# Score batches of two and three fills, a third one in the attention output's bank, and a scheduler with a readiness margin

## The reference

```
x  = layer_norm(x)                                   # entry norm
q,k,v,z_a,B,C,h,z_c = split(x @ w_in, 8)             # w_in 1024 x 4096, each part 512 wide
y_att  = chunk_attention(q,k,v,rel_bias) * silu(z_a) # 8 heads of 64; chunks of 64 frames;
                                                     # a chunk sees itself and 8 chunks before
y_conv = B * conv3(C*h) * silu(z_c)                  # causal depthwise conv of width 3
out = layer_norm(2**0.25 * x + concat(y_att, y_conv) @ w_out)
```

## Time and profile before

| | |
|---|---|
| median of 3 runs | 1316.02 us (1315.36 to 1316.21) |
| profiled execution | 1315.51 us |
| its span on the slowest core (core 2), first to last instruction | 1313.9 us |
| spans of the 8 cores | 1311.1 to 1313.9 us, granted PE clock 0.994 to 0.998 of full speed |
| PE busy | 1264.3 us (96%), 8146 matmuls recorded |
| DVE busy | 943.1 us (72%) |
| ACT busy | 731.4 us (56%) |
| POOL busy | 529.5 us (40%) |
| chain that ended last | PE 89% |

### The profile page before, as it was taken

The page is one execution under the profiler, slowest core; times in us unless marked ns, Lnnn a source line. Parts: engine busy times, 40 slices in busy tenths (PEclk is TensorE's granted clock), DMA queues, the critical chain, the costliest instruction groups (busy, mean ns, idle before and its releaser), DMA issues.

```text
span 1313.9 us, 27380 instructions; the slowest of 8 cores (1311.1 to 1313.9 us)
## 1 busy us (share of the span) xinstructions
PE 1264.3 (96%) x8146; PEld 594.9 (45%) x8308; DVE 943.1 (72%) x1671; ACT 731.4 (56%) x1082; POOL 529.5 (40%) x880
## 2 busy tenths in 40 slices
PE   5989999999999999999999999999999999999996
PEld 3434444444444444444444444444444444444443
DVE  2488987858678685876858688585885868676377
ACT  4665555555545565654654556465564565555563
POOL 4555533424343342433524334243443334334244
PEclk9999999999999999999999999999999999999998
DMA  9993313323222331222312323131222313221012
GB/s 290 322 254 113 88 55 93 89 49 89 58 77 79 87 89 25 88 83 73 89 41 73 89 74 96 59 87 41 83 87 73 89 43 89 69 76 49 13 70 73
DMA packets 126001, 117.16 MB, mean 89 GB/s; under 512 B 103200, under 2 KB 103200, under 8 KB 125728
## 3 DMA queue, kind: packets, MB, share of 16 engines
q1 hardware_dynamic: 125856, 115.40, 30.8%
HBM read 57.69 MB, written 33.55 MB: 69 GB/s over the span
## 4 chain that ended last, share of the span: by engine, by line
PE 89%; issue 3%; DMA 3%; DVE 2%; POOL 2%; ACT 1%; SPq 1%; POOLq 0%; DVEq 0%; ACTq 0%
PE mm L646 45%; PE mm L657 17%; PE mm L760 15%; PE pv L967 6%; PE sc L911 5%; DMA cst_sb<-cst 1%; DMA out<-xs 1%; DMA xs<-x 1%; DMA xnT<-xhb 0%; PE mm L833 0%; POOL pvs L985 0%; DVE stats L528 0%; DVE PT L951 0%; ACT xhb L855 0%; POOL rstd L538 0%
## 5 line engine op out<-in xcount | busy, mean ns | idle before, releaser
L646 PE MATMUL mm<-xnT,w_in_sb 128*128 128x512 bf16 x2970 | 709.3, 379 | 9.2 <-DVE tz L710 3.7
L646 PEld LDWEIGHTS mm<-xnT,w_in_sb 128*128 128x128 bf16 x3072 | 285.5, 98 | 300.6 <-issue 29.5
L924 ACT ACTIVATE PT<-sc 128x1024 bf16<-128x1024 f32 (+1 forms) x288 | 275.9, 999 | 115.6 <-PE sc L911 110.9
L657 PE MATMUL mm<-w_in_sb,xnT 128*128 128x512 bf16 x996 | 237.9, 379 | 1.9 <-issue 1.1
L760 PE MATMUL mm<-w_out_sb,yT 128*128 128x512 bf16 x929 | 221.5, 379 | 1.9 <-issue 1.3
L967 PE MATMUL pv<-vA,PT 128*128 128x65 bf16 x2240 | 203.3, 193 | 10.8 <-POOL PT L936 3.8
L967 PEld LDWEIGHTS pv<-vA,PT 128*128 128x128 bf16 x2240 | 150.2, 97 | 126.2 <-issue 18.6
L951 DVE TENSOR_TENSOR PT<-PT,etab 128x512 bf16<-128x512 bf16 (+1 forms) x304 | 123.6, 429 | 95.2 <-POOL PT L936 51.9
L985 POOL TENSOR_TENSOR pvs<-pvs,rden 128x256 f32<-128x256 f32 x128 | 100.7, 786 | 193.3 <-DVE rden L984 152.4
L657 PEld LDWEIGHTS mm<-w_in_sb,xnT 128*128 128x128 bf16 x1024 | 95.4, 98 | 105.7 <-issue 9.5
L766 DVE SCALAR_TENSOR_TENSOR xs<-xs,mm 128x512 f32<-128x512 f32 x120 | 82.2, 685 | 70.1 <-PE mm L760 59.1
(11 more groups left out here) (88 smaller groups left out, 1147.1 us busy)
## 6 DMA issues: line engine op xcount, KB each, us to landing
xs<-x SPq DMA_DIRECT2D x64, 512.0 KB, 3.6
out<-xs SPq DMA_DIRECT2D x60, 512.0 KB, 2.8
xs<-w_in SPq DMA_DIRECT2D x20, 512.0 KB, 12.8
g1bc_sb<-w_in SPq DMA_DIRECT2D x4, 512.0 KB, 12.7
b1bc_sb<-w_in SPq DMA_DIRECT2D x4, 512.0 KB, 12.8
vA<-w_in SPq DMA_DIRECT2D x4, 512.0 KB, 13.1
yT<-ytok SPq DMA_TRANSPOSE x128, 2.3
out<-xs SPq DMA_DIRECT2D x8, 256.0 KB, 2.0
```

Source lines behind the costliest of these rows:

```text
L646: P.op("pe", lambda e, i=i, kc=kc: e.matmul(mm[i][:, :], lhsT=w_in_sb[:, kc, c0:c0 + 128], rhs=xnT[:, sl, kc, :], start=(kc == 0), stop=(k ...
L657: P.op("pe", lambda e, i=i, kc=kc, t=t, c0=c0: e.matmul(mm[i][:, :], lhsT=xnT[:, sl, kc, t * 128:(t + 1) * 128], rhs=w_in_sb[:, kc, c0:c0 ...
L924: P.op("act", lambda e, x=x, sp=sp, w=w: e.activation(out=PT[:, sp, :, 0:w], in_=sc[x][:, :, 0:w], func=AF.Exp, scale=0.125), reads=["sc%d ...
```

## The change

Four things are changed together.

1. The PSUM banks are laid out anew. There are three score buffers `sc0`, `sc1`, `sc2` of two banks each and two `mm` banks. The two banks of `sc2` are also the third `mm` buffer and `pv`. A pair's five fills are now made in two batches: the first two in `sc0` and `sc1`, the last three in `sc2`, `sc0`, `sc1`. That is eight batches a block, and four in a block that starts a sequence. `pick` keeps units off the third `mm` buffer when their position lies from 14 before to 9 behind a batch of three; `place` moves such a batch by up to 12 positions (a position is one unit matmul) to where, by its count, the units are delayed least.
2. The scheduler's assumed times are changed: latencies between engines, durations on POOL, the DMA rate. A released operation that isn't PE's counts as ready later by 0.2 of what its deadline lies beyond 8 us, at most 3 us behind a DMA and 0.3 us behind an engine's operation. Zeroing the corner of `PT` may go to POOL or DVE.
3. The last output projection: its first two units leave out their last k chunk at first (that of the last convolution output) and add it after both have done the other seven. The last tile is made in units of 512, 256 and 256 columns, and its layer norm takes mean and variance with `bn_stats` on DVE instead of with ACT's squares; DVE finishes both halves.
4. Casts of weights and tables keep their choice of ACT or POOL; with the new assumed times, 19 of the 40 weight casts stand on ACT, where 7 stood before.

```diff
+FRAC = 0.5
+BEFORE = 14
+AFTER = 9
-LAT = 0.1
-DMA_MB = 0.3
+HOLD = {"pe": 0.0, "act": -0.09, "dve": -0.08, "pool": 0.17, "sp": 0.0}
+def lat(a, b):
+    if b == "pe":
+        return 0.145
+    return 0.16 if "pool" in (a, b) else 0.1
+DMA_MB = 0.31
+RISK = {"dma": 3.0, "sp": 1.5, "op": 0.3, "share": 0.2, "free": 8.0}
...
-                    ready[m] = max(ready[m], end + LAT)
-                    solid[m] = max(solid[m], end + LAT)
+                    to = nodes[m]["eng"]
+                    r = end + lat(e, to)
+                    if to != "pe":
+                        most = RISK["dma"] if e == "sp" else RISK["sp"] if to == "sp" else RISK["op"]
+                        r += min(most, max(0.0, RISK["share"] * (nodes[m]["alap"] - r - RISK["free"])))
+                    ready[m] = max(ready[m], r)
+                    solid[m] = max(solid[m], r)
...
-    mm = [ps("mm%d" % i, [128, 512], F32) for i in range(NMM)]
+    sc = [ps("sc%d" % i, [128, 2, 512], F32) for i in range(3)]
+    mm = [ps("mm%d" % i, [128, 512], F32) for i in range(2)] + [sc[2][:, 0, :]]
-    sc = [ps("sc%d" % i, [128, 2, 512], F32) for i in range(2)]
-    pv = ps("pv", [128, 2, 2, 65], F32)
+    pv = sc[2][:, 1, 0:260].rearrange("p (a b c) -> p a b c", a=2, b=2)
+    scr = [["sc0"], ["sc1"], ["mm2", "pv"]]
...
+    def pick(ord_, p):
+        for i in ord_:
+            if i < 2 or not any(p - AFTER < w < p + BEFORE for w in wide):
+                break
+        ord_.remove(i)
+        ord_.append(i)
+        return i
...
-                    P.op("pool", lambda e, sp=sp, c0=c0: e.memset(PT[0:64, sp, :, c0:c0 + 64], 0.0),
-                         writes=rs, us=0.2)
+                    fn = lambda e, sp=sp, c0=c0: e.memset(PT[0:64, sp, :, c0:c0 + 64], 0.0)
+                    P.any_op({"pool": (fn, 0.2), "dve": (fn, 0.2)}, writes=rs)
...
-        nbat = (len(fl) + 1) // 2
-        S = 8 * nu / nbat if nxt is not None else 8 * (nu - LU) / (nbat + 0.3)
+        S = 8 * nu / 4 if nxt is not None else 8 * (nu - LU) / 4.15
-        for k in range(nbat):
-            at(k * S, lambda k=k: qk_batch(fl[2 * k:2 * k + 2], b))
         for p in range(4):
-            z = max(n for n, f in enumerate(fl) if f[0] == p) // 2 * S
+            mine = [f for f in fl if f[0] == p]
+            z = p * S
+            if has_prev:
+                at(z, lambda two=mine[:2]: qk_batch(two, b))
+            z += FRAC * S
+            z = place(units, z, p * S + 8)
+            at(z, lambda three=mine[-3:]: qk_batch(three, b))
...
+    def o_last(b):
+        order = (4, 5, 6, 0, 1, 2, 3, 7)
+        pair = [next_mm(), next_mm()]
+        for hf in range(2):
+            o_mm(b, 0, pair[hf], hf * 512, 512, order[:7], True, False)
+        for hf in range(2):
+            o_mm(b, 0, pair[hf], hf * 512, 512, order[7:], False, True)
+            o_sum(b, 0, hf, pair[hf])
+        ln1_last(b, 0)
...
+        for k, (c0, w) in enumerate(((0, 512), (512, 256), (768, 256))):
+            i = next_mm()
+            o_mm(b, t, i, c0, w, order, True, True)
+            P.op("dve", lambda e, i=i, c0=c0, w=w: e.tensor_tensor(
+                out=xs[:, s, c0:c0 + w], in0=xs[:, s, c0:c0 + w], in1=mm[i][:, 0:w], op=ALU.add),
...
+        ln1_end(b, t, s)
```

More of the change, by code:

```diff
@@ L824, in build, with o_mm @@
     ybuf = xnT[:, :, :, :].rearrange("p s k c -> p (s k c)").bitcast(F32).rearrange("p (t d) -> p t d", d=D)
-    def unit_O_last(b, t, hf):
+    def o_mm(b, t, i, c0, w, chunks, first, last):
+        for n, c in enumerate(chunks):
+            assert (yc_of[c - 4] if c >= 4 else yt_of[c // 2, t]) == b
+            P.op("pe", lambda e, c=c, n=n: e.matmul(
+                mm[i][:, 0:w], lhsT=yT[:, c, t * 128:(t + 1) * 128], rhs=w_out_sb[:, c, c0:c0 + w],
+                start=(first and n == 0), stop=(last and n == len(chunks) - 1)),
+                reads=["w_out%d" % c, ("yT%d_%d" % (c // 2, t)) if c < 4 else "yT%d" % c],
+                writes=["mm%d" % i], us=w / 2400.0 + 0.0024)
+            pos_now[0] += 1
+            pump_pv(3)
@@ L903, in qk_batch @@
         sl = b % 2
-        for x, (pair, grp) in enumerate(batch):
+        bank = [2, 0, 1] if len(batch) == 3 else [0, 1]
+        for x, (pair, grp) in zip(bank, batch):
             coff = 0
@@ L1052, in build, with gated, place @@
     acts = set()
+    slow = set()
+    def gated(g):
+        slow.add(id(g))
+        return g
+    def place(units, z, lowest):
+        best = None
+        for shift in (0, 2, -2, 4, -4, 6, -6, 8, -8, 10, -10, 12, -12):
+            w = z + shift
+            if w < lowest or w > 8 * len(units) - 4:
+                continue
+            wide.append(base[0] + w)
+            ord_, late = list(mmo), 0.0
+            free = [0.0] * NMM
+            for n, g in enumerate(units):
+                p = 8.0 * n
+                i = pick(ord_, base[0] + p)
+                start = max(p + late, free[i])
+                if p - 8 < w <= p:
+                    late += max(0.0, free[2] - w - late)
+                    free[2] = w + late + 9
+                    start = max(p + late, free[i])
+                late = start - p
+                free[i] = start + 8 + (9.5 if id(g) in slow else 6)
+            late += 0.002 * abs(shift)
+            wide.pop()
+            if best is None or late < best[0]:
+                best = (late, w)
+        wide.append(base[0] + best[1])
+        return best[1]
     def block(b):
```

107 lines of the change are left out of this document (66 added, 41 removed).

## The result

The changed kernel takes 1302.13 us, the median of 4 runs (1301.55 to 1303.1), against 1316.08 us (1315.36 to 1316.21, 4 runs) before: ratio 0.9894, 95% interval 0.9879 to 0.9908. Forecast were 1300.7 us, 1294 to 1309. The sum was nearly right; of its terms one was right, two were too large, one had the wrong sign and one was missing.

A forecast was written before the change was run, and what follows sets the result against it. The prediction took PE as the bound, with next to nothing left to wait for. Its terms -9.0 + 1.5 - 7.2 - 0.6 = -15.3 us gave 1300.2 from the profiled 1315.5, so a median of 1300.7 us, range 1294 to 1309.

The forecast's parts named there:

- The runs of score matmuls: On PE, 45 fewer runs of score matmuls, each costing 0.2 us whatever its length: -9.0 us.
- The price of three: At the 64 batches of three, PE sometimes waits for the shared bank's evacuation: +1.5 us, bounds 0 and 16.
- The waits: Nine PE waits behind the first matmuls partly go, less 2.5 us for new ones: -7.2 us, bounds -12.6 and +5.
- the gate's: Two PE waits for a gate's evacuation, at 75.45 and 84.34 us, go: 4.0 us taken off.
- the pv buffer's: One PE wait for the pv buffer's evacuation, POOL being late with casts in between: 1.5 of 2.5 us taken off.
- the corner's waits: Five PE waits for the zeroed corner of PT, with 98 of 192 zeroings now on DVE: 3.0 of 4.6 us off.
- the bias product's: One PE wait for a bias product, behind statistics that wait for a load of x: 1.2 of 1.6 us off.
- I put back 2.5 us for new waits of the same kind: Allowance for new PE waits in the new order, set against the 9.7 us taken off: 2.5 us.
- PE gets to it after two units, so I leave 0.5 for it: Scaling of the second block's input comes later, behind the gate's evacuations: 0.5 us, within the 2.5 put back.
- The end: Last projection to program end: a 0.6 us wait goes and the rest stays 25.0 us; -0.6, bounds -4 and +2.
- Nothing but the runs: Rival: the waits are only moved, leaving the gains of -9.0 and -0.6: 1306.4 us, chance 0.22.
- ACT can't keep up: Rival: evacuations stand behind exponentials on ACT at batches of three, 16 to 22 us of PE waits: 1328.4 us, chance 0.08.

The follow-up runs named there:

- the batches alone: Changed kernel with the old scheduler numbers, zeroing on POOL and the old last projection: 1310.45 us, ratio 0.9949 to the kernel before.
- 64 runs put back: Changed kernel with each batch of three cut in two, its third fill one place later: 1316.01 us, ratio 0.9990 to the kernel before.
- without the margin: Changed kernel with no putting-off of ready times by deadline slack (share 0): slower than the kernel before, 16.3 us more lost on PE than in the changed kernel.
- loads earlier: Changed kernel with the weight loads' due times 3 us earlier: 1306.51 us, ratio 0.9922 to the kernel before.
- 1 MB more: Changed kernel with the two 0.5 MB residual-scaling tables also loaded once about 30 us after the start: 1312.0 us, ratio 0.9959 to the kernel before.
- tables held back: Changed kernel, margin off in PE's last 40 us, tables and w_out loads waiting for the second block's four input transposes: 1315.34 us, ratio 0.9984 to the kernel before.

## Why the prediction was right or wrong

- **The runs of score matmuls: right.** Predicted -9.0; -8.1 between the traces, -8.2 with the batches alone, 12.1 for 64 runs put back. An edge comes out at 0.18 to 0.19 us by these differences and at 0.21 at single places, which is the 0.20 assumed.
- **The price of three: wrong as a term of its own.** Predicted +1.5. In the changed kernel it is 0: no wait of PE from 160 to 1250 us. I argued from ACT's room and did not look at DVE, which evacuates the shared bank for the gates and for ubuf; without the margin the batch waited 10.4 us for it. Whether the price is paid is decided by what stands ahead of an evacuation, and the term belonged with the waits. On the Trainium skill, TensorEngine Tiling (Array Packing), section PSUM Bottleneck: between 550 and 630 us PE is busy for 80.00 of 80 with the larger batches, so no run here shows the reading of PSUM as a limit. Where a batch did wait for an evacuation, the evacuation itself took 0.68 us, and it was what stood ahead of it that made it late.
- **The waits: too large.** Predicted -7.2, and together with the price of three -5.7; measured -3.5. That the gate's, the pv buffer's and the corner's waits would go was right, two of them by causes read in the earlier trace rows; the bias product's stands elsewhere now, 1.8 us at 102.59. The step that failed is "I put back 2.5 us for new waits of the same kind". From 60 to 90 us PE lost 7.2 us where it had lost 3.9, so what went with the gate's waits was lost again, and 3.3 us more. One new wait, with the eight slow matmuls behind it, cost 5.8 us on the profiled core. The other seven cores show a second term that was too small, "PE gets to it after two units, so I leave 0.5 for it": PE waited 1.6 to 4.3 us there for the scaling L591, which was put behind the evacuations. I had looked in the order for what had stood ahead of the waiting operations, and not for the last w_in load on SP's queue, which the order already showed behind two transposes. And I priced waits at their length, where a wait of 4 us also costs the matmuls behind it their clock. The earlier trace rows did not warn of that, for on its core the clock stayed at 1.00. Other cores of the same trace do: on five of the eight it falls after the wait of 1.98 us for L710, to 0.81 to 0.88 on average from 70 to 78 us. On core 1:

```profile
74.00 8.32 PE L646 MATMUL mm<-xnT,w_in_sb 128*128 128x512 bf16 x30 [1.97 <-DVE tz L710]
```

  Thirty such matmuls take 6.6 us at the full clock, so the wait cost another 1.7 us there. One core's page is not the chip.
- **The end: wrong sign.** Predicted -0.6, measured +0.6. The wait for yT did go, and the new projection gave 0.4 us, less than can be told; the margin put 1.0 us on in this order, which I never looked for in the tail.
- **The head: missed.** -2.5 us. On DVE, L456 waits for the constants at the place where the last two nmr0 operations stand behind it; on POOL a cast stands ahead of the last two reciprocal roots. Before, POOL in order of time:

```profile
13.60 1.04 POOL L484 CAST w_in_sb<-xs 128x1024 bf16<-128x1024 f32 x1 [2.42 <-DMA xs<-w_in]
14.80 0.22 POOL L535 TENSOR_SCALAR rstd<-mv 128x1 f32<-128x1 f32 x1 [0.16 <-POOL w_in_sb L484]
```

  and after:

```profile
11.77 0.22 POOL L562 TENSOR_SCALAR rstd<-mv 128x1 f32<-128x1 f32 x1 [0.87 <-DVE mv L560]
12.14 0.57 POOL L565 TENSOR_TENSOR rstd<-rstd,nhalf 128x1 f32<-128x1 f32 x1
14.05 0.22 POOL L562 TENSOR_SCALAR rstd<-mv 128x1 f32<-128x1 f32 x1 [1.35 <-DVE mv L560]
```

  The largest wait of PE in the whole trace, 11 us before its first matmul, was the one that I took as given. With only this changed the kernel is slower, so the 2.5 us count in this order and not by right.
- **The rivals.** "Nothing but the runs" (1306.4) was wrong because the scheduler gave the head and the losses behind 120 us; in the ramp it was right, the waits were only moved; "ACT can't keep up" did not come, though its figure of 16 us is nearly what the kernel without a margin lost, on DVE instead of ACT.

The errors were +0.9, -1.5, +3.7, +1.2 and -2.5. Their sum is 1.8 us by the cores' medians, and the forecast of 1300.7 was 1.4 us off: by luck better than its parts, since a head that I had not forecast paid for most of the waits.

What stays open is which order is good before 110 us. The three others tried there (loads earlier, 1 MB more, tables held back) lost 13.7 to 22.0 us in all against 9.3, each at its own places. The best ramp of all runs here is that of the kernel without a margin, 6.6 us from 60 to 120 us, in the kernel that loses most behind it.

## What to carry to other kernels

Count the edges of small matmul runs: in the ten kernels here with 112 or 113 runs PE's work without the lost was 1245.2 to 1247.0 us, while the lost went from 9.3 to 26.1. In a list-scheduled kernel, read the order on each queue and engine for what stands ahead of every operation that PE will wait for, DMA queue included, and do not sum the waits that vanish without asking which comes next: mending one place moved the loss to the next within 5 us. Keep far-off work from standing ahead of an evacuation: with the shared bank in place the margin that does this was worth 16 us, and it cost 2 us from 60 to 120 us, where it held a load back. Read more than one core: the slowest core's longest wait was not that of the other seven.
